# Seven buffers in place of ten in the ring that receives the gathered expert rows

## The chip, the core and the metric

The kernel runs on one core of one Trainium2 chip. A core has five engines that run their own instruction lists and meet at semaphores: TensorE (PE in the profile; its weight loads are PEld), VectorE (DVE), ScalarE (ACT), GpSimd (POOL) and SyncE (SP). Transfers between the device memory and the on-chip memory are carried by 16 DMA engines that belong to the core. The metric is the device time of one launch in microseconds (us); lower is better.

## What is computed

The reference is one decoder block on 1024 tokens of width 1024: a modulation, a mixing part (a state-space group beside an attention group) and a retrieval part over 16384 single-neuron experts. The change lies in the retrieval part. For each token, 8 heads pick 16 experts each, which is 128 experts for a token; each expert is one row of `expert_down` (dotted with the token) and one row of `expert_up` (added up with a weight).

```
def chunk_fn(hc):
    q = (hc @ w_query).reshape(TOKEN_CHUNK, PEER_HEADS, 2, PEER_HALF)
    s = jnp.einsum('thpd,pkd->thpk', q, sub_keys)
    s1, i1 = lax.top_k(s[:, :, 0], PEER_TOPK)
    s2, i2 = lax.top_k(s[:, :, 1], PEER_TOPK)
    ...
    idx = e1 * PEER_N_KEYS + e2
    g = jax.nn.softmax(top_s, axis=-1).astype(hc.dtype)
    u = expert_down[idx]
    a = jax.nn.gelu(jnp.einsum('thkd,td->thk', u, hc))
    return jnp.einsum('thk,thkd->td', g * a, expert_up[idx])
```

The two tables lie side by side in device memory, so that one row of `experts` holds the down row and the up row of one expert: 2048 float32 numbers, 8 KB.

## The kernel before

The program runs six phases one after the other; the last, `phase_f`, starts with the output projection and then does the whole retrieval. It works in 1024 slots (`SLOTS`). The tokens come in 8 blocks of 128, one token to a partition, and a block has 128 slots, one for each of the 128 experts of a token. Slot n gathers one expert row for each of 128 tokens: 128 rows of 8 KB, 1 MiB.

A slot goes through these steps, each on its own engine:

- POOL issues the gather (line 1329) into `pair[n % R]`, one buffer of a ring of R buffers. Four of the buffers are called `pair_a` in the profile, the others `pair_b`. From gather number R on, POOL first waits (`hold(pool, up_used, n + 1 - R)`) until TensorE has used up gather n - R, whose buffer is needed.
- DVE waits for the gather's own semaphore and dots the down half with the tokens (`dot`, line 1585).
- ACT takes the gelu of the dot product (`gelu`, line 1449).
- DVE multiplies it with the softmax weight (`weight`, line 1579). In DVE's program the weight of slot n - 2 stands ahead of the dot of slot n (`LAG = 2`).
- ACT scales the up half of the buffer in place (`scale_up`, line 1453).
- TensorE adds the scaled half up in its accumulators with 8 transposing matmuls (`add_up`, line 1372). The last of them counts up `up_used`, which frees the buffer.

Between these slots the engines do other work at places written down by hand in tables of slot numbers. There are 64 tasks, one for each head of each block. For a task, TensorE computes the queries (line 1354) and the scores (line 1363), and DVE finds the best experts in six parts (lines 1509 to 1548), one part behind a dot. At 16 slots of the loop (`WEIGHED`, just ahead of slots 24, 56, 88, 128, 192 and every 64 after that up to 896) DVE and ACT also make the softmax weights of a batch of tasks: ACT's exponential there (line 1445) stands ahead of the gelu of the same slot. At each block's start the tokens of a later block are turned for the queries (lines 1343 and 1436). Tasks are searched ahead of their use, so this other work ends some 128 slots before the last slot. SP fetches the query weights `wq` early in the phase, and per block it fetches a stored 512 KB of `x2` and writes 512 KB of output.

Of the kernel before, what the change touches and what calls it, by code (L numbers as in the profile page):

```python
# [1204 lines left out]


def phase_f(nc, A, S):
    R, NA = 10, 16
    LAG = 2
    LOWEST = -3.0e38  # L1210
    PARTS = 6
# [446 lines left out]
def program(nc, A):  # L1658
    S = Store(nc)
    for phase in (phase_a, phase_b, phase_c, phase_d, phase_e, phase_f):  # L1660
        phase(nc, A, S)
# [18 lines left out]
```

## Time and profile before

| what | value |
|---|---|
| time, median of 3 runs | 3476.82 us (3476.23 to 3476.93) |
| the profiled execution, its own time | 3474.86 us |
| its span, first to last instruction | 3473.1 us |
| busy: PE, DVE, ACT, POOL | 71%, 66%, 46%, 39% |
| first gather issued, last gather dotted | 825.5 us, 3460.9 us from the span's start |

The span is what the profile's rows add up to; some 2 us lie around it. Gathers fill the last three quarters of the span. A wait in the profile is written as the idle time in front of an instruction and what ended it: `[1.17 <-DMA pair_b...]` says that the engine stood idle for 1.17 us until that transfer had landed. Rows of DMA activity are cut into 40 equal slices of the stretch asked for; 16 engines together move about 421 GB/s when all are busy, one alone about 27.

### The profile page before, as it was taken

How to read it: one execution, taken by the hardware profiler on the slowest of the kernel's cores; microseconds unless marked ns; L12 is line 12 of the kernel's file. 1: busy time of each engine (PE TensorE's matmuls, PEld its weight loads, DVE VectorE, ACT ScalarE, POOL GpSimd, SP SyncE). 2: the span in 40 equal slices, each digit the busy share in tenths (PEclk: the TensorE clock that was granted, in tenths of full speed). 3: DMA queues.
4: the chain of work that ended last, by engine and by line, in shares of the span. 5: the costliest groups of instructions: out<-in, count | busy, mean ns of one | idle time of the engine just before them, and what ended most of it. 6: DMA issues, size and time to landing. Idle time of an engine off the chain costs nothing.

```text
span 3473.1 us, 39859 instructions
## 1 busy us (share of the span) xinstructions
PE 2472.4 (71%) x13357; PEld 1993.5 (57%) x13357; DVE 2302.5 (66%) x6276; ACT 1612.9 (46%) x2710; POOL 1356.5 (39%) x1165
## 2 busy tenths in 40 slices
PE   3597789995776677766666776766677766666666
PEld 1365457743666666665555565655666665555555
DVE  6835365436899777676777777777777677776554
ACT  3140243322555555554555555555545555555444
POOL 4203160001444444444444443444444444444564
PEclk8698988998888766776677777776766676776666
DMA  6410010025999999999999999999999999999997
GB/s 229 110 69 13 15 49 1 1 99 205 420 421 420 407 421 419 418 408 421 411 420 406 421 408 418 409 412 422 411 421 406 420 402 421 415 421 416 421 421 321
DMA packets 186477, 1143.51 MB, mean 329 GB/s; under 512 B 28832, under 2 KB 30751, under 8 KB 55199
## 3 DMA queue, kind: packets, MB, share of 16 engines
q0 software_dynamic: 147456, 1073.81, 74.8%
q1 hardware_dynamic: 31230, 66.24, 5.4%
q10 hardware_dynamic: 7584, 0.91, 0.2%
q8 instruction: 105, 1.72, 0.2%
q14 instruction: 102, 0.83, 0.1%
HBM read 1131.32 MB, written 8.39 MB: 328 GB/s over the span
## 4 chain that ended last, share of the span: by engine, by line
DMA 37%; DVE 18%; PE 10%; issue 8%; ACT 5%; POOL 1%; POOLq 0%; DVEq 0%; SPq 0%
DMA pair_b<-in_experts_dram,idx_g 23%; DMA pair_a<-in_experts_dram,idx_g 13%; DVE pair_b L1585 4%; PE outs L1372 3%; DVE pair_a L1585 3%; PE outa L1372 3%; ACT pair_b L1453 2%; PE outs L1397 2%; PE outa L1397 2%; ACT pair_a L1453 1%; PE pgg L1354 1%; DVE hot L1543 1%; DVE key L1545 1%; DMA wq<-in_w_query_dram 1%; DVE top_i L1510 1%
## 5 line engine op out<-in xcount | busy, mean ns | idle before, releaser
L1329 POOL DMA_INDIRECT pair_b<-in_experts_dram,idx_g x612 | 710.4, 1161 | 839.1 <-PE outs L1372 391.4
L1585 DVE SCALAR_TENSOR_TENSOR pair_b<-pair_b,h 128x1024 f32<-128x1024 f32 x612 | 749.0, 1224 | 416.2 <-DMA pair_b<-in_experts_dram,idx_g 399.9
L1453 ACT ACTIVATE pair_b<-pair_b,w 128x1024 f32<-128x1024 f32 x612 | 697.1, 1139 | 306.9 <-DVE w L1579 300.2
L1329 POOL DMA_INDIRECT pair_a<-in_experts_dram,idx_g x412 | 489.2, 1187 | 706.2 <-PE outs L1372 279.0
L1585 DVE SCALAR_TENSOR_TENSOR pair_a<-pair_a,h 128x1024 f32<-128x1024 f32 x412 | 504.1, 1224 | 279.6 <-DMA pair_a<-in_experts_dram,idx_g 272.1
L1372 PE MATMUL outa<-ident,pair_b 128*128 128x128 f32 x2448 | 477.7, 363 | 237.2 <-ACT pair_b L1453 230.6
L1372 PE MATMUL outs<-ident,pair_b 128*128 128x128 f32 x2448 | 448.6, 348 | 238.1 <-ACT pair_b L1453 234.5
L1372 PEld LDWEIGHTS outa<-ident,pair_b 128*128 128x128 f32 x2448 | 392.1, 189 | 316.9 <-ACT pair_b L1453 308.8
L1453 ACT ACTIVATE pair_a<-pair_a,w 128x1024 f32<-128x1024 f32 x412 | 469.3, 1139 | 206.0 <-DVE w L1579 206.0
L1372 PEld LDWEIGHTS outs<-ident,pair_b 128*128 128x128 f32 x2448 | 373.1, 181 | 305.7 <-ACT pair_b L1453 302.2
L1449 ACT ACTIVATE ga<-a 128x1 f32<-128x1 f32 x1024 | 206.8, 202 | 693.3 <-DVE pair_b L1585 401.6
L1372 PE MATMUL outa<-ident,pair_a 128*128 128x128 f32 x1648 | 326.7, 367 | 156.3 <-ACT pair_a L1453 155.6
L1372 PE MATMUL outs<-ident,pair_a 128*128 128x128 f32 x1648 | 305.3, 351 | 155.2 <-ACT pair_a L1453 151.7
L1372 PEld LDWEIGHTS outa<-ident,pair_a 128*128 128x128 f32 x1648 | 268.8, 191 | 209.9 <-ACT pair_a L1453 209.6
L1372 PEld LDWEIGHTS outs<-ident,pair_a 128*128 128x128 f32 x1648 | 254.6, 183 | 200.5 <-ACT pair_a L1453 196.9
L1354 PE MATMUL pgg<-h2t,wq 128*128 128x128 f32 x2048 | 251.4, 283 | 35.0 <-DMA wq<-in_w_query_dram 35.0
L1354 PEld LDWEIGHTS pgg<-h2t,wq 128*128 128x128 f32 x2048 | 247.4, 201 | 36.3 <-issue 36.3
L1579 DVE TENSOR_TENSOR w<-ga,g 128x1 f32<-128x1 f32 x1024 | 157.1, 153 | 39.3 <-ACT ga L1449 38.3
L1085 PEld LDWEIGHTS pee<-v,pts 128*128 128x128 f32 x576 | 83.7, 219 | 43.7 <-issue 26.6
L1175 ACT ACTIVATE pex<-scores,top 128x128 f32<-128x128 f32 (+7 forms) x64 | 47.4, 741 | 121.3 <-DVE top L1135 115.9
L1085 PE MATMUL pee<-v,pts 128*128 128x64 f32 x576 | 86.3, 302 | 18.8 <-DVE ya L1150 16.6
L1063 PE MATMUL scores<-kt,qt 96*128 96x512 f32 (+3 forms) x192 | 84.8, 557 | 1.8 <-PEq L841 1.8
(362 smaller groups left out, 2629.8 us busy)
## 6 DMA issues: line engine op xcount, KB each, us to landing
wada<-in_w_ada_dram SPq DMA_DIRECT2D x12, 2048.0 KB, 10.5
pair_b<-in_experts_dram,idx_g POOLq DMA_INDIRECT x612
wq<-in_w_query_dram SPq DMA_DIRECT2D x4, 2048.0 KB, 31.0
pair_a<-in_experts_dram,idx_g POOLq DMA_INDIRECT x412
xt<-in_x_dram SPq DMA_DIRECT2D x8, 512.0 KB, 6.2
wout<-in_w_out_dram SPq DMA_DIRECT2D x1, 4096.0 KB, 12.9
x<-in_x_dram SPq DMA_DIRECT2D x8, 512.0 KB, 7.6
out_dram<-x SPq DMA_DIRECT2D x8, 512.0 KB, 2.6
```

The source lines that it names most:

```text
L1063: last = t.matmul(sps[m % 2][:, a:b], S.qt[:, h, i * P:(i + 1) * P], S.kt[:, h, a:b], start=True, stop=True)
L1085: last = t.matmul(ob[:, h * DV:(h + 1) * DV], pts[:, m % 2, b * P:(b + 1) * P], S.v[:, b, h * DV:(h + 1) * DV], start=b == 0, stop=b == i)
L1175: s.activation(pex[:, m % 2, 0:n], sps[m % 2][:, 0:n], ACT.Exp, scale=SCALE, bias=top[:, m:m + 1], accum_out=rsum[:, m:m + 1]).then_inc(ex ...
L1329: p.indirect_dma_start(pair[n % R], None, A["experts"], bass.IndirectOffsetOnAxis(ap=idx[:, t % (2 * PH), k:k + 1], axis=0)).then_inc(pair ...
L1354: last = t.matmul(qb[:, n * P:(n + 1) * P], wq[:, PH // 2 - 1 - h // 2, k, (2 * (h % 2) + n) * PK:(2 * (h % 2) + n + 1) * PK], h2t[:, k, : ...
L1372: last = t.matmul(accs[i % 2][:, k * P:(k + 1) * P], pair[n % R][:, D + k * P:D + (k + 1) * P], S.ident[:], is_transpose=True, start=n % P ...
L1397: last = t.matmul(out[:, half * 512:(half + 1) * 512], src[:, k, tile(i)], wout[:, k0 + k, half * 512:(half + 1) * 512], start=k == 0, sto ...
L1449: s_.activation(ga[:, n % NA:n % NA + 1], a[:, n % NA:n % NA + 1], ACT.Gelu_apprx_tanh).then_inc(ga_ready, 1)
L1453: s_.activation(pair[n % R][:, D:], pair[n % R][:, D:], ACT.Copy, scale=w[:, n % NA:n % NA + 1]).then_inc(scaled, 1)
L1510: own.mark(v.max_index(out=top_i[:, n, 0:8], in_max=top_v[:, n, 0:8], in_values=sc))
L1579: v.tensor_tensor(w[:, n % NA:n % NA + 1], ga[:, n % NA:n % NA + 1], g[:, t, n % TOPK:n % TOPK + 1], ALU.mult).then_inc(w_ready, 1)
L1585: v.scalar_tensor_tensor(down, down, 1.0, S.h2[:, n // P, :], ALU.mult, ALU.mult, accum_out=a[:, n % NA:n % NA + 1]).then_inc(dotted, 1)
```

## The change

The ring has R = 7 buffers in place of 10. `pair_a` keeps its four, `pair_b` has three in place of six.

```
@@ -1205,7 +1205,7 @@
 def phase_f(nc, A, S):
-    R, NA = 10, 16
+    R, NA = 7, 16
     LAG = 2
     LOWEST = -3.0e38
     PARTS = 6
```

No instruction is added, taken away or put elsewhere on any engine. Which buffer a slot uses changes, and with it the point from which POOL waits, and what for. These are POOL's rows at the start of the gathers, in the kernel before; `g_upused` is the semaphore `up_used`.

```order
L1329 DMA pair_a<-in_experts_dram,idx_g 128x2048 [waits f_bd,g_idx]
L1329 DMA pair_a<-in_experts_dram,idx_g 128x2048 x3
L1329 DMA pair_b<-in_experts_dram,idx_g 128x2048 [waits f_h2,g_spill]
L1329 DMA pair_b<-in_experts_dram,idx_g 128x2048 x5
L1329 DMA pair_a<-in_experts_dram,idx_g 128x2048 [waits g_upused] x4
```

And the same place in the changed kernel:

```order
L1329 DMA pair_a<-in_experts_dram,idx_g 128x2048 [waits f_bd,g_idx]
L1329 DMA pair_a<-in_experts_dram,idx_g 128x2048 x3
L1329 DMA pair_b<-in_experts_dram,idx_g 128x2048 [waits f_h2,g_spill]
L1329 DMA pair_b<-in_experts_dram,idx_g 128x2048 x2
L1329 DMA pair_a<-in_experts_dram,idx_g 128x2048 [waits g_upused] x4
```

Seven gathers go out before POOL waits for TensorE's count, where it was ten, and from there on each gather waits for a slot seven back.

## Rows read from the trace of the kernel before

**Rows 1.** The profile's page, the gathers' queue: packets, MB, share.

```profile
q0 software_dynamic: 147456, 1073.81, 74.8%
```

**Rows 2.** Waits from 900 to 3440 us: us in total, times, longest.

```profile
DVE pair_b L1585 <- DMA pair_b<-in_experts_dram,idx_g: 392.3, 338, 2.4
POOL pair_b L1329 <- PE outs L1372: 390.7, 214, 5.6
```

**Rows 3.** Groups of DVE, 900 to 3440 us: count, busy, mean ns, idle.

```profile
L1579 DVE TENSOR_TENSOR w<-ga,g 128x1 f32<-128x1 f32 x996 | 152.8, 153 | 24.3 <-ACT ga L1449 23.3 <-issue 0.3
```

**Rows 4.** DMA queues, 900 to 3440 us: packets, MB, share.

```profile
q1 hardware_dynamic: 2016, 7.34, 0.7%
q8 instruction: 80, 1.31, 0.2%
```

**Rows 5.** Timeline of DVE the dots of slots 512 and 519.

```profile
2158.32 1.23 DVE L1585 SCALAR_TENSOR_TENSOR pair_a<-pair_a,h 128x1024 f32<-128x1024 f32 x1 [0.42 <-DMA pair_a<-in_experts_dram,idx_g]
...
2175.64 1.23 DVE L1585 SCALAR_TENSOR_TENSOR pair_b<-pair_b,h 128x1024 f32<-128x1024 f32 x1 [1.16 <-DMA pair_b<-in_experts_dram,idx_g]
```

**Rows 6.** DMA, 2170 to 2178 us in 40 slices: GB/s.

```profile
GB/s 369 451 328 369 451 410 451 451 410 410 328 205 205 205 82 82 82 41 41 287 328 82 123 123 410 410 287 369 410 369 532 369 410 532 246 410 164 287 328 246
```

**Rows 7.** DMA, 3453 to 3461 us, gathers' queue: packets, MB, share.

```profile
q0 software_dynamic: 28, 0.20, 5.9%
```

**Rows 8.** Chain that ended last: a gather from its issue to its landing.

```profile
2004.24 14.55 DMA pair_b<-in_experts_dram,idx_g
```

**Rows 9.** Timeline, the rest of slot 512's way to its release.

```profile
2157.75 1.28 ACT L1445 ACT_TABLE_LOAD   x1
...
2159.32 1.28 ACT L1449 ACT_TABLE_LOAD   x1
...
2165.77 4.88 PE L1354 MATMUL pgg<-h2t,wq 128*128 128x128 f32 x32
...
2172.30 0.94 POOL L1329 DMA_INDIRECT pair_a<-in_experts_dram,idx_g  x1 [4.48 <-PE outs L1372]
```

**Rows 10.** Line 1445: the first and last table load with their count.

```profile
L1445 ACT ACT_TABLE_LOAD x17: 1283/1283/1283, 830.0 to 3139.0; - x17
```

**Rows 11.** Timeline, dot and reissue of three slots: 128, 896, 457.

```profile
1176.68 1.22 DVE L1585 SCALAR_TENSOR_TENSOR pair_b<-pair_b,h 128x1024 f32<-128x1024 f32 x1
...
1191.88 0.94 POOL L1329 DMA_INDIRECT pair_b<-in_experts_dram,idx_g  x1 [5.33 <-PE outa L1372]
...
3139.10 1.22 DVE L1585 SCALAR_TENSOR_TENSOR pair_b<-pair_b,h 128x1024 f32<-128x1024 f32 x1
...
3149.03 1.88 POOL L1329 DMA_INDIRECT pair_b<-in_experts_dram,idx_g  x1 [0.45 <-issue]
...
2018.82 1.23 DVE L1585 SCALAR_TENSOR_TENSOR pair_b<-pair_b,h 128x1024 f32<-128x1024 f32 x1 [1.17 <-DMA pair_b<-in_experts_dram,idx_g]
...
2028.48 0.94 POOL L1329 DMA_INDIRECT pair_b<-in_experts_dram,idx_g  x1 [1.61 <-PE outa L1372]
```

**Rows 12.** Timeline, the first gather of all and the first after the pause.

```profile
825.50 1.16 POOL L1329 DMA_INDIRECT pair_a<-in_experts_dram,idx_g  x1 [124.69 <-PE outa L1397]
...
859.99 5.84 PE L1354 MATMUL pgg<-h2t,wq 128*128 128x128 f32 x32 [35.01 <-DMA wq<-in_w_query_dram]
...
867.49 1.00 POOL L1329 DMA_INDIRECT pair_a<-in_experts_dram,idx_g  x1 [22.28 <-PE outs L1372]
...
875.99 1.23 DVE L1585 SCALAR_TENSOR_TENSOR pair_a<-pair_a,h 128x1024 f32<-128x1024 f32 x1 [2.96 <-DMA pair_a<-in_experts_dram,idx_g]
```

**Rows 13.** DMA queues, 825 to 827.5 us (q0), 870 to 876 us (q1).

```profile
q0 software_dynamic: 7, 0.06, 16.5%
...
q1 hardware_dynamic: 379, 0.96, 42.0%
```

**Rows 14.** Windows of 5 us at the start: clock, DMA share, GB/s last.

```profile
860.00:865.00 5.00, 5.00 (x26) 5.00 (x27) 0.00 (x0) 0.00 (x0) 0.00 (x0) 0.57 1.03 390
865.00:870.00 5.00, 5.00 (x48) 5.00 (x47) 3.62 (x8) 4.13 (x9) 1.94 (x2) 1.00 1.05 386
```

More of the change, by code:

```diff
@@ L1207, in phase_f @@
 def phase_f(nc, A, S):
-    R, NA = 10, 16
+    R, NA = 7, 16
     LAG = 2
```

## The prediction

> **What bounds the kernel now.** I read the page first: the gathers' queue moves 1073.81 MB [rows 1], and no compute engine is over 71% busy. So the next view is the list of waits in the stretch of the gathers. DVE waits for gathers, and POOL waits for TensorE to free buffers [rows 2]. Both at once look like a ring that is too small, and the question is which of them sets the pace. The dots tell: DVE starts the dot of slot 512 at 2158.32 and that of slot 519 at 2175.64, both straight behind a landing [rows 5]. That is 17.32 us for seven slots, 2.47 to 2.48 us a slot. Over 900 to 3440 us there are 996 slots [rows 3], 2.55 us each. At 2.48 us they would take 2470 us; 7.34 MB of SP's transfers at 421 GB/s [rows 4] take 17 us more, and the last 53 us have the size of 80 instruction packets [rows 4] at under 1 us each. Hardly any time is left for an empty queue.
>
> But the 16 DMA engines are not alike. In 2170 to 2178 us the rate falls to 41 GB/s, one or two engines of 16, until the gather that POOL issues at 2172.30 reaches them [rows 6, 9], while the dots keep their pace [rows 5]. The others had run dry, and the slots were being finished by an engine that lags. The end shows it bare: from 3453 us on, 28 packets with 0.20 MB remain, at a share of 5.9% of 16 engines [rows 7]. That is one engine at work, and 0.20 MB are 24 rows of 8 KB where its share of a gather is 8: three gathers that the other fifteen have finished. A gather is landed when the slowest share is. So the bound is one lagging DMA engine, which is never empty now: a gather lands 14.55 us after its issue [rows 8], of which about 2.48 is their own transfer.
>
> **What the change does.** Nothing is issued more or less, so it costs nothing as long as that lagging engine has work. The ring fixes this: gather n + R can be issued when slot n is released. Let H be the time from the landing of slot n (where its dot starts) to the issue of gather n + R into its buffer, and L the time from issue to landing of a gather that has nothing queued ahead of it. The landing of n + R is late by
>
> H + L - R x 2.48 us, when that is positive.
>
> With ten buffers R x 2.48 is 24.8 us, with seven 17.36 us.
>
> *H.* Slot 457, a slot in a search by DVE: dot 2018.82, reissue 2028.48, H = 9.66 [rows 11]. I measured H the same way for 980 slots: from 6.0 to 15.2 us, the middle one 8.7, nine in ten under 10.1. The long ones lie at the softmax batches. Slot 512: the gelu waits for two table loads of 1.28 us around the exponential and can't start before 2160.60; TensorE does a stretch of query matmuls, 4.88 us, from 2165.77 on, ahead of this slot's `add_up`, and POOL issues at 2172.30 [rows 9]: H = 13.98 from the dot at 2158.32 [rows 5]. There are 17 such table loads, the last at 3139.0 [rows 10], 16 of them in the loop. Their slots (24, 56, 88, 128, 192, then every 64 to 896) have H = 12.1, 12.2, 12.6, 15.2, 12.1, 13.2, 13.1, 13.9, 12.6, 14.0, 13.6, 13.2, 14.1, 14.4, 12.3, 9.9; that of 128 is 1191.88 less 1176.68, that of 896 3149.03 less 3139.10 [rows 11].
>
> *L.* No gather before meets an empty lagging engine, so I bound it. From below: the first gather is issued at 825.50 [rows 12] and only seven packets have started by 827.5 [rows 13], so data starts no sooner than about 1.9 us after issue; with 2.48 us of transfer, L is at least 4.3. From above: after the pause a gather is issued at 867.49 and dotted at 875.99, with DVE waiting for it [rows 12], 8.50 us, with `wq` still flowing: 0.96 MB of it after 870 us [rows 13], 2.3 us at 421 GB/s. Without that, 6.2. The upper end has foreign work in it that I can size, so I take **L = 6.0**.
>
> The Trainium skill, "DMA: Bandwidth & Descriptors", section "Anatomy of one DMA — SWDGE (gpsimd) path", gives a gather from POOL a fixed 2.0 us plus its bytes over 436 GB/s, 4.4 us for 1 MiB. By that the loss would be about 5 us and not measurable; the trace, at 6.2 us after the pause, speaks for more.
>
> *The sum.* With L = 6.0 a slot is late when H is over 11.36. The first fifteen batch slots are over it, by .7, .8, 1.2, 3.8, .7, 1.8, 1.7, 2.5, 1.2, 2.6, 2.2, 1.8, 2.7, 3.0 and .9: 27.6 us. At 128, 320, 384, 640 and 704 the next seven landings took longer than 17.36 us anyway, up to 18.5, because of an instruction packet; that cover takes off 4.5: 23. Of the other slots a few in the searches and right behind the batches add 3. Each delay moves everything behind it, so they add up: **+26 us**, 0.75%. Adding each slot's lateness over the whole trace, with every delay carried on, gives 26 too; the same with L = 4.3 gives 5, with 5.3 15, with 7.0 45, with 8.5 120.
>
> *Edits at nothing.* The start: PE waits 35.01 us for `wq` until 859.99 with all ten buffers full [rows 12]. With three gathers fewer ahead of it `wq` comes some 7 us sooner, POOL resumes some 7 us sooner, and the DMA engines are busy meanwhile, at 390 and 386 GB/s [rows 14]. What they don't move before the pause they move after it, so this hides nothing and costs nothing, if the refill comes before they run dry. The other waits (the searches' results for POOL, DVE's and SP's waits at block ends) are for slots far ahead or behind.
>
> Sum against the profiled execution: 3474.86 + 26 = 3501. The median of the runs is 2.0 above that execution, so the forecast is 3503.
>
> **The rivals.**
>
> *No change to be measured (within 0.2%, 7 us).* The lagging engine restarts as quickly as the lower bound lets it, L up to 4.5: then only slots with H over 12.9 lose, about 5 us, 3482. For it speak the dips in which 15 engines restart together, from 41 to 287 GB/s within 1.5 us of POOL's issue [rows 6, 9]. Against it speaks the landing after the pause. That the change does nothing at all, because ten is never used, is out: POOL waits for TensorE in most slots [rows 2].
>
> *Much slower: the searches gate too.* A search slot has H = 9.66 [rows 11], so from L = 7.7 on all 62 searches lose some slots. POOL's issue itself takes 0.94 us in some rows and 1.88 in others [rows 11], which could put L at 7.0 and the loss at 45, 3522; at 8.5 it would be 120, 3597, but that has `wq` in it.
>
> *Faster.* At the start the two waits for `wq` and for the first release end 7 us earlier. That gains if the DMA engines have idle time there to give back: the rates of 390 and 386 in place of 421 [rows 14] are worth 0.8 us over all 16. If they meant that the one lagging engine idles, all of the 7 us could come back: 3470. It decides only where the batches lose less than that, so at an L under 4.6.
>
> **How the numbers follow.** Slower at the batches as summed: 0.67; the searches gating as well: 0.15; no change: 0.14; faster: 0.04. A difference of 0.2%, 7 us, is about what a measurement of this kernel can tell from none. The likeliest case's own range is L from 5.3 to 6.5, +14 to +35: 3491 to 3512. The range for 8 in 10 reaches into both neighbours: from 3483 (L = 4.5) to 3524 (L = 7). Slower 0.82, same 0.14, faster 0.04.
>
> **What would show it.** In the changed kernel the dots should keep their 2.48 us between the batches, and behind each batch slot, seven slots later, one dot should come 1 to 4 us late with DVE waiting for its gather; DMA rate there should fall to nothing for that time, where now 41 GB/s remain. Issue to landing in the chain should be some 7 to 8 us in ordinary slots. The last DMA engine should end less far behind the others. The prediction is wrong if dots are late in the searches as well (L too low), or if no dot is late after a batch, or if H itself grows with the smaller ring.

## The result, and the profile of the changed kernel

| kernel | time, median of 4 runs | ratio to before (95% interval) |
|---|---|---|
| before, ring of ten | 3476.53 us (3474.07 to 3476.93) | 1 |
| changed, ring of seven | 3541.73 us (3532.65 to 3548.41) | 1.0187 (1.0160 to 1.0215) |

The change costs 65 us. The forecast was 3503 us with a range to 3524: the direction was right, the size was less than half. The profiled execution took 3536.73 us with a span of 3534.9, so its rows have 62 us more than those of before to explain.

These are lines of the page of the changed kernel: the span, what the DMA engines moved in each of 40 slices, and the gathers' queue with its packets, MB and share of 16 engines.

```profile
span 3534.9 us, 39862 instructions
...
GB/s 225 130 46 13 15 48 1 30 74 275 391 399 394 396 416 402 411 403 418 395 413 391 403 402 403 410 396 418 389 414 395 410 399 408 401 407 410 420 415 352
...
q0 software_dynamic: 147456, 1073.81, 74.6%
```

The last line answers to [rows 1], and it holds the first surprise. The packets and bytes are the same. But 74.6% of 3534.9 us is 2637 us of work for each engine, where 74.8% of 3473.1 us was 2598. (The shares are given to 0.1%, which is some 3 us.) So some 39 of the 62 us are not idle engines: the same rows took longer to move. Only about 23 us are added idle time.

The waits, engine and line, from 900 to 3440 us, answer to [rows 2]:

```profile
DVE pair_a L1585 <- DMA pair_a<-in_experts_dram,idx_g: 403.0, 318, 3.6
...
POOL pair_a L1329 <- PE outs L1372: 370.7, 207, 4.5
...
DVE pair_b L1585 <- DMA pair_b<-in_experts_dram,idx_g: 306.6, 239, 3.5
```

The longest wait of DVE for a gather has grown from 2.4 us [rows 2] to 3.6 us; `pair_a` now holds four of seven buffers, so its sums grow and those of `pair_b` shrink. The same stretch by DMA queues answers to [rows 4]; the first line is the gathers':

```profile
q0 software_dynamic: 139814, 1018.16, 98.5%
q1 hardware_dynamic: 2016, 7.34, 0.7%
q8 instruction: 79, 1.29, 0.2%
```

At 1.0486 MB a slot these are 971 slots in 2540 us, 2.62 us each, against 2.55 before.

The batch at slot 512, which the prediction worked through, looks like this now. These are the timeline's rows of its dot, of the two gathers that POOL issues when slots 512 and 513 are released, of the dots of slots 516 and 517 between them, and of the dots of slots 519 and 520, which wait for those two gathers.

```profile
2190.61 1.22 DVE L1585 SCALAR_TENSOR_TENSOR pair_a<-pair_a,h 128x1024 f32<-128x1024 f32 x1
...
2201.11 1.23 DVE L1585 SCALAR_TENSOR_TENSOR pair_b<-pair_b,h 128x1024 f32<-128x1024 f32 x1 [1.52 <-DMA pair_b<-in_experts_dram,idx_g]
...
2204.76 0.94 POOL L1329 DMA_INDIRECT pair_a<-in_experts_dram,idx_g  x1 [4.35 <-PE outs L1372]
...
2205.17 1.23 DVE L1585 SCALAR_TENSOR_TENSOR pair_b<-pair_b,h 128x1024 f32<-128x1024 f32 x1 [2.76 <-DMA pair_b<-in_experts_dram,idx_g]
...
2206.00 1.21 POOL L1329 DMA_INDIRECT pair_a<-in_experts_dram,idx_g  x1 [0.30 <-PE outs L1372]
...
2210.41 1.23 DVE L1585 SCALAR_TENSOR_TENSOR pair_a<-pair_a,h 128x1024 f32<-128x1024 f32 x1 [1.47 <-DMA pair_a<-in_experts_dram,idx_g]
...
2215.13 1.23 DVE L1585 SCALAR_TENSOR_TENSOR pair_a<-pair_a,h 128x1024 f32<-128x1024 f32 x1 [3.41 <-DMA pair_a<-in_experts_dram,idx_g]
```

H is 2204.76 less 2190.61, 14.15 us; before it was 13.98. L is 2210.41 less 2204.76, 5.65 us, near the 6.0 taken. Slot 519 comes 19.80 us after slot 512 where it was 17.32 [rows 5]: 2.5 us late, as forecast. Part of that had built up two slots before: the dot of slot 517 starts 4.06 us behind that of 516. By the sum it should not be late, for its gather went out at 2196.57, 11.1 us after slot 510 had landed, and the sum charges nothing under 11.36. And slot 520, whose gather went out only 1.24 us after that of 519, comes 4.72 us behind it and not 2.48. That is another 2.2 us, which the sum did not have. An instruction packet (16 KB on the profile's instruction queue, about 1 us of one engine) falls into this one; it is too short to be all of the 2.2.

DMA from 2203 to 2211 us in 40 slices of 0.2 us:

```profile
DMA  3995999979764211193288697979999898955666
GB/s 123 492 492 246 492 410 410 492 328 492 328 287 205 123 41 82 82 492 82 123 205 328 246 410 328 492 328 492 410 410 492 328 246 205 287 205 164 287 246 287
```

The rate falls to 41 GB/s at 2205.8, as in [rows 6]. Two things differ. When the gather of 2204.76 arrives, it comes back for one slice, at 2206.4, and falls to 82 and 123 again before it runs full. And it falls again to between 164 and 287 from 2209.4 on, although the gather of 2206.00 had been issued more than 3 us before. (Engines that run full make 421.)

### The profile page after: what moved, and what is told of

The parts are those of the page before. It is cut to its first block, busy times and chain, and to the rows that moved or that the text cites. A ratio compares the mean times of both kernels' runs of the same rounds, so it can differ in the third digit from the quotient of the medians.

```text
span 3534.9 us, 39862 instructions
## 1 busy us (share of the span) xinstructions
PE 2490.8 (70%) x13357; PEld 2001.8 (57%) x13357; DVE 2300.3 (65%) x6276; ACT 1613.8 (46%) x2710; POOL 1363.5 (39%) x1165
## 3 DMA queue, kind: packets, MB, share of 16 engines
q0 software_dynamic: 147456, 1073.81, 74.6%
## 4 chain that ended last, share of the span: by engine, by line
DMA 29%; DVE 18%; PE 17%; issue 10%; ACT 6%; POOL 1%; POOLq 0%; DVEq 0%; SPq 0%
DMA pair_a<-in_experts_dram,idx_g 14%; DMA pair_b<-in_experts_dram,idx_g 14%; PE pgg L1354 5%; PE outa L1372 4%; PE outs L1372 4%; DVE pair_a L1585 4%; DVE pair_b L1585 3%; ACT pair_a L1453 2%; ACT pair_b L1453 2%; PE outs L1397 2%; PE outa L1397 2%; DVE top_i L1510 1%; DVE top_i L1513 1%; DVE top_v L1512 1%; DVE s L1511 1%
## 5 line engine op out<-in xcount | busy, mean ns | idle before, releaser
L1329 POOL DMA_INDIRECT pair_a<-in_experts_dram,idx_g x586 | 696.7, 1189 | 961.5 <-PE outs L1372 396.5
L1585 DVE SCALAR_TENSOR_TENSOR pair_a<-pair_a,h 128x1024 f32<-128x1024 f32 x586 | 717.3, 1224 | 437.9 <-DMA pair_a<-in_experts_dram,idx_g 437.1
L1453 ACT ACTIVATE pair_a<-pair_a,w 128x1024 f32<-128x1024 f32 x586 | 667.5, 1139 | 292.2 <-DVE w L1579 292.2
L1329 POOL DMA_INDIRECT pair_b<-in_experts_dram,idx_g x438 | 510.1, 1165 | 646.9 <-PE outs L1372 309.7
L1585 DVE SCALAR_TENSOR_TENSOR pair_b<-pair_b,h 128x1024 f32<-128x1024 f32 x438 | 536.0, 1224 | 325.1 <-DMA pair_b<-in_experts_dram,idx_g 324.3
L1372 PE MATMUL outa<-ident,pair_a 128*128 128x128 f32 x2352 | 464.8, 366 | 239.9 <-ACT pair_a L1453 238.8
L1453 ACT ACTIVATE pair_b<-pair_b,w 128x1024 f32<-128x1024 f32 x438 | 499.0, 1139 | 220.4 <-DVE w L1579 220.4
L1372 PE MATMUL outs<-ident,pair_a 128*128 128x128 f32 x2336 | 434.2, 350 | 227.9 <-ACT pair_a L1453 226.5
L1372 PE MATMUL outa<-ident,pair_b 128*128 128x128 f32 x1744 | 344.6, 365 | 174.8 <-ACT pair_b L1453 174.3
L1372 PE MATMUL outs<-ident,pair_b 128*128 128x128 f32 x1760 | 331.0, 353 | 192.0 <-ACT pair_b L1453 190.7
```

Of the source, the lines that this page charges most:

```text
L1329: p.indirect_dma_start(pair[n % R], None, A["experts"], bass.IndirectOffsetOnAxis(ap=idx[:, t % (2 * PH), k:k + 1], axis=0)).then_inc(pair ...
L1372: last = t.matmul(accs[i % 2][:, k * P:(k + 1) * P], pair[n % R][:, D + k * P:D + (k + 1) * P], S.ident[:], is_transpose=True, start=n % P ...
L1453: s_.activation(pair[n % R][:, D:], pair[n % R][:, D:], ACT.Copy, scale=w[:, n % NA:n % NA + 1]).then_inc(scaled, 1)
L1585: v.scalar_tensor_tensor(down, down, 1.0, S.h2[:, n // P, :], ALU.mult, ALU.mult, accum_out=a[:, n % NA:n % NA + 1]).then_inc(dotted, 1)
```

## The experiments

The runs named by a ratio with its interval are medians of 4 to 11 executions beside 13 to 21 of the kernel before on the same chip; the ring of six and the table of runs by gathers in flight are one profiled execution each. "Slot time" below is the span less 837 us (825 ahead of the first gather, 12 behind the last dot) over 1024 slots; "engine time" is the gathers' share of the span, again over 1024. Before has 2.574 us and 2.537 us.

**Is it the number of gathers ahead, or the buffers?** The ring keeps ten buffers, and POOL waits as if there were seven.

```
-                if n >= R:
-                    hold(pool, up_used, n + 1 - R)
+                if n >= 7:
+                    hold(pool, up_used, n + 1 - 7)
```

> Ten buffers stay where they were, but from gather 7 on POOL waits until TensorE has used up the gather seven back. Theory A (what costs is how far ahead gathers may be issued, nothing else): the same time as the ring of seven, 3530 to 3550 us. Theory B (part of the cost is where the buffers lie, or that a buffer and its semaphore come back sooner): clearly under 3530, down to 3477.

Measured: 3534.11 us, ratio 1.0165 (1.0148 to 1.0182), an interval that overlaps that of the ring of seven (1.0160 to 1.0215). That is 59 us over before. Theory A holds. Where the buffers lie, and how soon one comes back, costs nothing that shows; POOL's point of issue makes the loss.

**The batches.** The exponential's table loads are taken out of the ring of seven.

```
-                s_.activation(g[:, at:to, :], g[:, at:to, :], ACT.Exp).then_inc(exp_ready, 1)
+                s_.activation(g[:, at:to, :], g[:, at:to, :], ACT.Copy).then_inc(exp_ready, 1)
```

> Ring of seven; ACT copies in place of the exponential of the softmax weights, so that line 1445 and the gelu behind it load no table (the softmax weights are wrong numbers; all else is as it was). It shortens the hold of the batch slots by up to 2.6 us. Theory A (the loss comes from the 16 batches, where the hold is longest and all engines run dry): the excess of 62 us over before falls to 10 to 30 us, 3487 to 3507. Rival (the loss is spread over all slots, because any engine's hiccup now shows): at most 16 x 0.5 us comes back, over 3525.

Measured: 3502.05 us, 1.0074 (1.0057 to 1.0090). More than half of the loss comes back for a few us of hold at 16 places, so the batches carry the larger part. But 27 us stay, where the hold of the batch slots is now at most 11.6 us by the trace, and 8.8 to 10.4 in all but one. By the prediction's sum that leaves little to pay for. Most of these 27 us lie away from the batches (the section on the prediction says how that is summed).

**The hold of every slot.** In the ring of seven the weight follows one slot behind.

```
-    LAG = 2
+    LAG = 1
```

> Ring of seven; the weight of slot n - 1 instead of n - 2 stands ahead of the dot of slot n, so a buffer is held about one slot (2.5 us) less. Theory A (hold plus empty-queue latency against 17.36 us): the excess nearly goes, 3474 to 3490. Rival (fewer than ten in flight costs in itself, whatever the hold): stays over 3520. A cost of its own is possible where DVE now waits for the gelu of the slot before, some 3 us at each of 16 batches if it isn't hidden.

Measured: 3491.75 us, 1.0046 (1.0029 to 1.0062), a little above the top of what Theory A expected. Three quarters of the loss go. What stays is at the batches, where the gelu still stands behind the table loads: summed in the same way, the slots around the batches lose 31 us more than before, and the others none. These are ACT's two table loads at the batch of slot 512 there, and POOL's issue behind that slot's release:

```profile
2171.21 1.28 ACT L1445 ACT_TABLE_LOAD   x1
...
2172.78 1.28 ACT L1449 ACT_TABLE_LOAD   x1
...
2184.59 1.94 POOL L1329 DMA_INDIRECT pair_a<-in_experts_dram,idx_g  x1 [5.21 <-PE outs L1372]
```

POOL still stands idle for 5.21 us there until TensorE releases a buffer.

**Both at once.**

> Ring of seven with both shortenings of the hold: the weight one slot behind, and no exponential at the batches (the softmax weights are wrong numbers). If the loss is the hold against the ring's length, both parts together leave nothing: 3470 to 3480. If the two cover the same 45 us each, about 3490 as with the lag alone.

Measured: 3475.57 us, 0.9990 (0.9981 to 1.0000): level with before. With both parts of the hold shortened, seven buffers lose nothing. One alone takes away 38 us of the 65, the other 48; that is more than 65 together, so the two overlap in part.

**One buffer more.** `R, NA = 8, 16`.

> Ring of eight. By the prediction's sum (H + L - 19.84 us, L = 6.0) it costs about 1 us: 3477 to 3480. Rival (a restart from a dry queue costs more than L, and dry spells begin before the lateness shows): 3485 to 3505.

Measured: 3475.17 us, 1.0003 (0.9994 to 1.0013), 0.4 us over before on this chip. That is a little under what was expected, and the 1 us of the sum is too small to be told from it. The rival falls. So there is a steep step between eight and seven.

**One buffer less.** `R, NA = 6, 16`.

> Ring of six. The prediction's sum over the trace of before gives +131 us for L = 6.0, +174 for 6.5, +222 for 7.0: 3606, 3649, 3697. If a dry spell costs more than the sum says by the same factor as with seven (62 for 26), 3750 to 3800.

Measured: 3786.06 us against 3474.81 on the same chip, 311 us more, in the range that was expected by scaling with the factor of the ring of seven. The sum itself fails again. That is 2.4 times the prediction's sum for L = 6.0, as it was 2.4 times with seven (62 for 26), and 1.4 times the sum for L = 7.0. The page's line of the gathers' queue in this run:

```profile
span 3784.3 us, 39863 instructions
...
q0 software_dynamic: 147456, 1073.81, 74.0%
```

74.0% of 3784.3 us is 2800 us for each engine, 202 more than before. Two thirds of the loss are rows that take longer.

**L by itself, and what a queue is worth.** Now the ring keeps its ten buffers and POOL additionally waits for the landing of the gather k slots back, so that at most k are in flight:

```
                 if n >= R:
                     hold(pool, up_used, n + 1 - R)
+                if n >= k:
+                    hold(pool, pair_in[(n - k) % R], 16 * ((n - k) // R + 1))
```

> Ten buffers, but POOL issues a gather only when the one before it has landed, so no gather ever has another ahead of it: the slot's time is L, from issue to landing, plus the wake-up of POOL. If L is 6.0 us as the prediction took it, 1024 slots end near 825 + 6140 + 12 = 6980 us; if L is 6.5, near 7490; at the lower bound of 4.3, 5240.

> Ten buffers, a gather is issued when the one two before it has landed. If a gather costs L when alone and 2.48 us behind another, the slot's time is L / 2: 3.0 us for L = 6.0, 3920 us in all; 3.25 for 6.5, 4170. If the transfers themselves are slower when little is queued, more than that.

> Ten buffers, a gather is issued when the one three before it has landed. Sum of the prediction: L = 6.0 to 6.5 is under 3 x 2.48 = 7.44 us, so the DMA engines never wait and the time stays within 10 us of before (one DMA engine's lead can't build up, which by this sum costs nothing). Rival (gathers with a short queue ahead are slower, or each engine's own hiccup now delays the slot): 3500 to 3700.

> Ten buffers, a gather is issued when the one four before it has landed. One, two and three in flight gave 6.72, 3.44 and 2.90 us a slot, where L alone was 5.9. New theory (a gather that has too little queued ahead of it starts with slow rows on every engine, and the ring of seven has about four in flight): four in flight is near the pace of the ring of seven, 2.53 to 2.65 us a slot, 3480 to 3600 us, with more engine time than before. Rival (the loss of the ring of seven is idle engines behind the batches alone): 2.48 to 2.50 us a slot, no more than 10 us above before.

> Five in flight. New theory: the ring of eight, which lost nothing, has about five in flight, so this is within 10 us of before, 3475 to 3485. Rival (each landing that POOL waits for costs something whatever the depth): clearly above that.

| run | time | slot time | engine time | slow rows in a gather |
|---|---|---|---|---|
| one in flight | 7721.48 us | 6.72 us | 3.10 us | 14.6 |
| two | 4376.02 us | 3.45 us | 3.02 us | 12.6 |
| three | 3816.54 us | 2.91 us | 2.78 us | 5.9 |
| four | 3471.11 us | 2.57 us | 2.55 us | 0.8 |
| five | 3473.18 us | 2.57 us | 2.55 us | 0.8 |

The last column counts, in the traces, the rows of a gather's 128 that took over 0.6 us, where an ordinary one takes 0.31. Before has 0.6 of them, the ring of seven 1.5, the ring of six 4.9.

The expectations did badly here, and each miss says something. With one in flight 6980 us was expected for L = 6.0, and 7721 came: the wake-up of POOL had been named but not counted. With two it is over both sums, which the expectation had put down to slower transfers. With three the prediction's sum said no loss at all, and even the rival stopped at 3700 us, where 3817 came. With four, the new theory expected the slower pace of the ring of seven, and it was wrong: four cost nothing. Five came out as expected.

With one in flight POOL issues every 6.6 to 6.7 us. Two of its rows, each with the idle time until the landing:

```profile
3006.25 1.30 POOL L1331 DMA_INDIRECT pair_b<-in_experts_dram,idx_g  x1 [5.29 <-DMA pair_a<-in_experts_dram,idx_g]
3012.89 1.30 POOL L1331 DMA_INDIRECT pair_b<-in_experts_dram,idx_g  x1 [5.33 <-DMA pair_b<-in_experts_dram,idx_g]
```

The landings' semaphores, read from the trace for 800 of these slots, stand 5.90 us behind the issue (the middle one), and POOL needs some 0.8 us to go on. So L is 5.9, next to the prediction's 6.0. Between these two issues DMA shows one gather alone, in slices of 0.17 us:

```profile
DMA  0000000000009823099889969989994200000000
GB/s 0 0 0 0 0 0 0 0 0 0 0 0 493 148 49 148 0 444 345 247 345 345 444 296 493 444 345 493 444 493 197 99 0 0 0 0 0 0 0 0
...
q0 software_dynamic: 144, 1.05, 46.6%
```

Data starts 2.0 us behind the issue, then the rate falls to next to nothing for nearly a microsecond, and only then runs full. The share is 46.6% of 6.64 us, 3.09 us of engine time for 8 rows and a completion, where before it took 2.54. The slow rows are the first ones: over 800 gathers of this run, the nine rows that start first take 0.88 us each on average, the sixteenth still 0.59, and from about the fiftieth on a row takes 0.31. With 16 engines and 14.6 slow rows in a gather, that fits the first row of each engine.

With three in flight the simple sum fails most plainly. Three slots are 7.44 us, more than 5.9 + 0.8, so no engine should wait; yet a slot takes 2.91 us. These are the windows 1400 to 1600 us of the runs with three and with four in flight (the last three numbers are the granted clock, the DMA share and GB/s):

```profile
1400.00:1600.00 200.00, 128.67 (x731) 110.45 (x730) 120.94 (x348) 92.75 (x147) 91.21 (x69) 0.70 0.97 362
```

```profile
1400.00:1600.00 200.00, 140.00 (x820) 121.50 (x820) 143.98 (x416) 104.36 (x167) 104.19 (x78) 0.72 1.01 417
```

The engines are busy for 0.97 of the time with three in flight and move 362 GB/s in it; with four they are busy for 1.01 and move 417. The share differs by 4%, the rate by 15%. A queue of three keeps the engines busy and slow.

**Four in flight, timed.**

> Four in flight out of ten buffers again, now timed. If four in flight are all that the DMA engines need, it is level with before, within 0.1%. If the single 3471 us was real and a shallow queue of four also helps something (SP's transfers and the instruction packets find a shorter queue), it is 0.1 to 0.3% faster. If four is just at the edge, some runs are slower than before.

Measured: 3472.14 us, ratio 0.9987 (0.9978 to 0.9996). Four are enough, and the kernel is a very little faster than before, which has five to eight in flight when POOL issues. Why it is faster was not tried; the shorter queue for SP's transfers and the instruction packets, which the expectation names, is a guess.

**Ten buffers with the weight one slot behind.** `LAG = 1` in the kernel before.

> Ring of ten with the weight one slot behind. If ten buffers are enough, a shorter hold gives nothing, 3470 to 3478; if before still pays for slow rows at its batches, up to 10 us come back.

Measured: 3475.4 us, 0.9991 (0.9982 to 1.0000). Nothing to speak of is left in the hold when there are ten buffers.

## Why the prediction was off

**What bounds the kernel: right in the main.** The gathers' transfer does, and at the end one engine lags. That the same engine sets the pace all along was not shown: the traces don't name the engine of a row. The end of the changed kernel's gathers bears out one more item of the forecast. This is the rate from 3514 to 3523 us in 40 slices:

```profile
GB/s 437 401 473 400 400 401 437 437 401 437 437 364 437 510 364 400 437 473 364 437 437 364 291 182 109 109 109 73 73 73 73 36 36 0 0 0 0 0 0 0
```

The rate is under 200 GB/s from 3519.2 us on and nothing from 3521.4: the last engine lags by some 2 us, where three gathers, 7.4 us, were left to it before [rows 7].

**H and L: right, L in part by luck.** H is as it was: taken from the landing's semaphore over the whole trace, the middle slot has 9.0 us before and 8.9 now. (The prediction took the dot for the landing, which gave 8.7; in some slots the dot comes later.) L alone is 5.9, from the run with one gather in flight. The 6.0 was read off the landing after the pause, with 2.3 us of other work taken off it as an estimate. What L is made of was not seen: the lower bound of 4.3 took 2.48 us of transfer for a gather with nothing ahead of it, where the engines work for 3.1. The range ended at 3524 for L = 7, where the prediction's own sum gives 3522; nothing hangs on that.

**Where: mostly right.** I summed what each slot's landing took beyond 2.475 us in the two traces, from slot 20 on: 76.8 us before, 139.5 now. In the 14 slots around each of the 16 batches it is 14.5 us before and 65.2 now, 51 more; in all other slots 12 more. The forecast had 23 and 3. The same sum for the ring of seven without table loads has 8 more than before around the batches and some 25 more elsewhere; with the weight one slot behind it has 31 more around the batches and 11 less elsewhere.

**The signs.** The dots keep their pace between the batches, and are late behind them. Two signs did not come: the rate does not fall to nothing behind the batch of slot 512 but to the 41 GB/s it had before, and a gather lands 9.6 us after its issue in the middle slot, where 7 to 8 were expected.

**The start: right.** POOL's first issue behind the pause is at 859.42 us in place of 867.49 [rows 12], 8 us sooner, and there is no gain from it: the twentieth gather lands 74.0 us behind the first issue, where it was 73.8.

**The step that failed** is the first sentence of the costing, that the smaller ring "costs nothing as long as that lagging engine has work", and with it the formula that charges H + L - R x 2.48 and takes 2.48 us for every gather behind the first. The term that it puts at nothing is what a gather costs when few are queued ahead of it. The runs show that the gathers need four in flight to keep the pace of before. With three a slot takes 0.34 us more, of which 0.23 is engine time and not idleness, with two 0.88, half of it engine time. So the loss begins before a landing is late by the formula, as at slot 517 above. In the ring of seven the room between H and the ring's 17.36 us decides how many there are: 17.36 - 8.9 = 8.5 us, 3.4 slots, and behind a batch of H = 14 only 1.4. I counted, at each of 970 issues, the gathers that had not landed yet, the new one included:

| kernel | two or fewer | three | four | more | priced | measured |
|---|---|---|---|---|---|---|
| before | 0 | 0 | 0 | 970 | 0 | 0 |
| ring of eight | 0 | 22 | 149 | 799 | 7 | 0 |
| ring of seven | 14 | 149 | 566 | 241 | 63 | 65 |
| seven, no table loads | 0 | 99 | 617 | 254 | 34 | 27 |
| seven, weight one slot behind | 13 | 31 | 180 | 746 | 25 | 17 |
| seven, both | 0 | 3 | 146 | 821 | 1 | -3 |
| ring of six | 23 | 570 | 375 | 2 | 214 | 311 |

"Priced" takes the slot times of the table above against 2.57: 0.34 us for an issue with three in flight, 0.88 for two (one issue of the fifth row has one in flight, 4.1 us); "measured" is the time over before of the same chips. Ten buffers held seven back have 4, 151 and 571, priced 55, measured 59. The order is right but among the three that lose next to nothing, and the sizes are within some 10 us, but for the ring of six, where a third is missing. The counts can be off by a few, because some landing records are missing from most of the traces. The price of a count of three is not exact, since the paced runs hold it for good while a ring drifts in and out of it.

The slow rows make the same account in another way. The rows over 0.6 us, counted beyond 0.31 us each in slots 20 to 1000, add 32 us to every engine's time in the ring of seven over what they add before, most of the 39 us of longer work; in the ring of six it is some 160 of 202.

So the mechanism of the forecast, a hold that is too long for the ring, is confirmed by the runs that shorten it. What was mis-sized is the price of a short queue: 26 us for the gathers that come late by L alone, against the 62 found. The rival "the searches gate too" gave 45 us for the wrong reason (L = 7.0). The low end, L = 4.3, is out: the trace of one gather in flight gives 5.9. So is the estimate of 4.4 us for 1 MiB from the formula of the Trainium skill, "DMA: Bandwidth & Descriptors", section "Anatomy of one DMA — SWDGE (gpsimd) path".

**What stays open.** Why three in flight are not enough, when three slots are more time than one gather needs, is not shown. The traces show that the time goes into slow rows, and they hint at which: 30 ns before a slow row starts, 14.1 transfers of over 1 KB are under way on average in the run with three in flight, before any other row 15.8; with one in flight it is 7.1 and 15.7. So slow rows tend to start when some engine has just stood idle. One reading fits this and the count of slow rows: a row is slow where its engine restarts from an empty queue. POOL issues only when the slowest engine's share of a gather has landed, and the faster engines can have run dry by the time the next rows reach them, with three in flight now and then, with one every time. The trace doesn't say which engine moved a row, so this is argued and not shown, and no run tried it.

## What to carry to other kernels

Ask of a ring of buffers not only whether the last buffer comes back before the transfer engines run dry, but how many transfers are in flight at each issue: the ring's length in slots, less the hold in slots. Measure first how many the engines need for their full rate, by making the issuer wait for the k-th landing back; it is one line and one run for each k. Here the middle hold is 3.6 slots, and with four in flight that makes 7.6 buffers: eight lost nothing, although their long holds left fewer than four in flight at 22 issues, and seven lost 1.9%. Much of such a loss is engine time, which the busy share does not show as idleness.

## What the runs showed of the hardware that was not expected

- One 1 MiB gather of 128 rows of 8 KB lands 5.9 us after POOL's issue when it is alone. The first 16 rows to start take 0.91 down to 0.59 us there, on average, in place of 0.31. With one, two, three and four in flight a slot takes 6.72, 3.45, 2.91 and 2.57 us; a fifth adds nothing.
- DMA engines can be busy for 0.97 of a stretch and move 362 GB/s, or for 1.01 and move 417, with the same transfers. The share of busy time was no measure of the rate here.
- Four in flight were 0.13% faster than the ring of ten with its five to eight (0.04 to 0.22%).
